# A tile arena moved by 56 columns, and another order of transposes and gate products at the end of an rwkv stage

## The reference

```
y = ((y - mean) * rsqrt(var + GN_EPS)).reshape(b, s, d) * ln_w + ln_b
bonus = sum(rh * kh * r_k, -1, keepdims=True) * vh
y = y + bonus.reshape(b, s, d)
return (y * g) @ w_o
```

## Time and profile before

| | |
|---|---|
| runs, median of three | 1237.35 us (1236.31 to 1237.88) |
| the profiled execution | 1236.65 us |
| its span | 1234.8 us |
| TensorE busy | 1221.0 us, 99% |
| VectorE, ScalarE, GpSimd busy | 538.0, 608.5, 776.7 us |
| instructions | 23237 |

### The profile page before, as it was taken

How to read it: one execution, slowest core, us unless ns; L and a number is a source line. 1 busy time by engine, 2 the same in 40 slices (tenths; PEclk the granted TensorE clock), 3 DMA queues, 4 the chain that set the end, 5 groups by cost and what they waited for, 6 DMA issues and landing times.

```text
span 1234.8 us, 23237 instructions
## 1 busy us (share of the span) xinstructions
PE 1221.0 (99%) x9698; PEld 1062.6 (86%) x9698; DVE 538.0 (44%) x819; ACT 608.5 (49%) x796; POOL 776.7 (63%) x200
## 2 busy tenths in 40 slices
PE   8999999999999999999999999999999999999998
PEld 7888887788988888899898888888888998888887
DVE  4432234655333333343523333348986573332233
ACT  7454443545554444585565445464422444554442
POOL 3988880153288888767369888843016525888884
PEclk9999999999999999999999999999999999999999
DMA  8655554253255555554235555542341133555551
GB/s 301 212 186 199 178 201 148 89 184 140 103 174 201 202 175 200 193 184 160 103 137 202 176 201 179 195 170 103 136 163 44 38 117 122 184 195 197 180 201 68
DMA packets 31020, 202.01 MB, mean 164 GB/s; under 512 B 3424, under 2 KB 5344, under 8 KB 7392
## 3 DMA queue, kind: packets, MB, share of 16 engines
q1 hardware_dynamic: 28064, 196.63, 45.2%
q10 hardware_dynamic: 2880, 4.26, 1.0%
HBM read 198.79 MB, written 2.10 MB: 163 GB/s over the span
## 4 chain that ended last, share of the span: by engine, by line
PE 95%; ACT 1%; POOL 1%; issue 1%; DVE 1%; DMA 1%; SPq 0%; POOLq 0%; DVEq 0%; ACTq 0%
PE psum L353 25%; PE psum L355 13%; PE psum L344 10%; PE psum L346 10%; PE psum L345 10%; PE psum L986 6%; PE psum L999 3%; PE psum L2992 2%; PE psum L3008 1%; POOL wlo L3371 1%; PE psum L2847 1%; PE psum L341 1%; PE psum L343 1%; PE psum L342 1%; PE psum L2962 1%
## 5 line engine op out<-in xcount | busy, mean ns | idle before, releaser
L3371 POOL TENSOR_TENSOR wlo<-raw,whi 128x2048 fp32r<-128x2048 f32 x160 | 734.3, 4595 | 289.7 <-ACT whi L314 244.3
L353 PE MATMUL psum<-f_both,whi 128*128 128x512 f32 x1408 | 497.3, 394 | 1.0 <-DVE wlo L699 1.0
L314 ACT ACTIVATE whi<-raw 128x2048 fp32r<-128x2048 f32 x160 | 306.3, 1915 | 223.1 <-PE psum L355 173.9
L355 PE MATMUL psum<-f_both,wlo 128*128 128x256 f32 x1408 | 397.4, 282 | 0.0
L353 PEld LDWEIGHTS psum<-f_both,whi 128*128 128x128 f32 x1408 | 264.4, 188 | 62.0 <-DVE wlo L699 1.6
L355 PEld LDWEIGHTS psum<-f_both,wlo 128*128 128x128 f32 x1408 | 264.7, 188 | 1.5
L344 PE MATMUL psum<-whi,ahi 128*128 128x512 f32 x352 | 137.2, 390 | 0.2 <-POOL wlo L3371 0.2
L346 PE MATMUL psum<-whi,alo 128*128 128x512 f32 x352 | 137.0, 389 | 0.0
L345 PE MATMUL psum<-wlo,ahi 128*128 128x512 f32 x352 | 137.0, 389 | 0.0
L909 DVE TENSOR_TENSOR psum<-psum,arena 128x512 f32<-128x512 f32 x43 | 30.1, 700 | 239.7 <-ACT arena L625 239.6
L925 DVE TENSOR_TENSOR alo<-arena,ahi 128x512 fp32r<-128x512 f32 x44 | 98.7, 2244 | 31.7 <-ACT ahi L858 31.7
(11 more groups left out here) (425 smaller groups left out, 1474.1 us busy)
## 6 DMA issues: line engine op xcount, KB each, us to landing
raw<-stream SPq DMA_DIRECT2D x182, 1024.0 KB, 4.8
con<-consts SPq DMA_DIRECT2D x1, 1376.0 KB, 14.2
x<-x_in SPq DMA_DIRECT2D x1, 1024.0 KB, 4.9
raw<-stream SPq DMA_DIRECT2D x2, 512.0 KB, 6.9
kept_x<-x ACTq DMA_DIRECT2D x1, 1024.0 KB, 3.9
x<-kept_x ACTq DMA_DIRECT2D x2, 512.0 KB, 4.7
out<-x SPq DMA_DIRECT2D x4, 256.0 KB, 2.0
arena<-gm_w_s ACTq DMA_DIRECT2D x1, 512.0 KB
```

Of the source, the lines that this page charges most:

```text
L314: nc.scalar.activation(whi[:, slot, :], raw[:, c % RAW, :], ACT.Copy).then_inc(high_made, 1)
L353: nc.tensor.matmul(psum[:, bank, :].rearrange("p (a n) -> p a n", a=2), whi[w], f_both[:, :, k, :], start=k == 0, stop=False, skip_group_c ...
L355: return nc.tensor.matmul(psum[:, bank, 0:TOK], wlo[w], f_hi[:, k, :], start=False, stop=k == KT - 1, skip_group_check=True)
L3371: nc.gpsimd.tensor_tensor(part(wlo[:, slot, :]), part(raw[:, c % RAW, :]), part(whi[:, slot, :]).bitcast(F32), ALU.subtract)\
```

## The change

Three edits. The unused columns ahead of the arena are 16 in place of 72, which puts it at byte 103968 of each partition. On VectorE `gated(3)` stands ahead of `y_low(2)`. On TensorE `turned(2)` stands amid the tiles of `out_tiles(1)`, which takes a list of tiles for this; each of the two calls waits for the same value of `rw_ylo`.

```diff
-        sb("up_to_line", [P, 72])
+        sb("up_to_line", [P, 16])
...
             whole(3)
+            gated(3)
             y_low(2)
-            gated(3)
             y_low(3)
...
-            def out_tiles(w):
+            def out_tiles(w, tiles=range(4)):
 
                 m, q = PASSES[w]
                 eng.wait_ge(s("rw_ylo"), w + 1)
-                return pair_tiles("rw_o", range(4 * q, 4 * q + 4), 0, m, last=KT - 1)
+                return pair_tiles("rw_o", [4 * q + k for k in tiles], 0, m, last=KT - 1)
...
             out_tiles(0)
-            out_tiles(1)
+            out_tiles(1, (0, 1))
             turned(2)
+            out_tiles(1, (2, 3))
             turned(3)
             out_tiles(2)
             out_tiles(3).then_inc(chunk_used, 2)
```

## The result

The changed kernel takes 1229.01 us (median of 6 runs, 1228.64 to 1231.48), the kernel before 1236.76 (6 runs): a ratio of 0.9941, interval [0.9928, 0.9954]. A second series gave 1230.23 against 1236.59, 0.9947 [0.9934, 0.9961]. The profiled execution took 1229.58 us, with a span of 1227.8.

A forecast was written before the change was run, and what follows sets the result against it. TensorE, busy 99% of the span, was taken as the bound. 2.17 + 1.54 - 0.70 + 0.35 = 3.36 us gained, the arena zero; from a median of 1237.35 to 1234.0 us, range 1231.0 to 1237.0.

The forecast's parts named there:

- Parts 1 and 2: End of rwkv: gated(3) ahead of y_low(2) on VectorE, turned(2) amid TensorE's second products; together 3.36 us earlier.
- last product: End of rwkv on TensorE: the stage's last product starts at 37.68 in place of 41.04.
- second products: End of rwkv: TensorE reaches these at 24.73 in place of 26.90, 2.17 us gained, and ends them at 30.41.
- first low part's product: First last_out product that waits for GpSimd's low part: that part is ready at 31.11, TensorE comes at 30.41.
- The new wait: TensorE, ahead of the first last_out product: 0.70 us of waiting for GpSimd's low part, which had cover before.
- the 1.54 us of the lower clock: Second products at the end of rwkv: 1.54 us read as the lower clock's price, gained once the idle time goes.
- Rival A: End of rwkv: TensorE's clock still falls, the 1.54 us come back, 2.2 gained in all, 1235.2 us; chance 0.10.
- Part 3: Arena 56 columns lower, at byte 103968, 32 past a multiple of 256: effect on reads taken as zero.
- rival C: FFN matmuls reading f_both: the arena move ends reads slowed by their place beside the weights; 1 ns gives 2.8 us; chance 0.09.
- The bound of 11.3 us: Limit on the arena's effect, either way: 4 ns on each of 2816 matmuls that read f_both; given little weight.
- the second objection: Caveat on the rows used for the arena's zero: their matmuls are not of the fp32r kind that f_both is.
- Both rows give no loss: Reason for little weight on the arena's bound: sums and lw, 32 bytes past a multiple of 256, read no slower.

The follow-up runs named there:

- e1: The kernel before with only the arena moved (16 unused columns in place of 72), orders unchanged: 1232.17 us, beside 1236.49 for the kernel before.
- e2: The changed kernel with 72 unused columns again, so only the new order of gated(3) and turned(2): 1233.74 us, 0.9975 of the kernel before.
- e7: The changed kernel with 56 unused columns added ahead of raw, weights 224 bytes up, arena back at byte 104192: 1229.97 us.
- e9: The changed kernel with 8 unused columns ahead of raw (weights 32 bytes up) and 8 ahead of the arena, which stays at byte 103968: 1234.86 us.
- e14: The changed kernel with 32 unused columns ahead of the arena in place of 16, distance of f_both to the weights +96 mod 256: 1230.3 us.
- e15: The changed kernel with 40 unused columns ahead of the arena in place of 16, distance of f_both to the weights +128 mod 256: 1238.5 us.
- e5: The changed kernel, arena still at byte 103968, but f_both alone 32 bytes below it at 103936: 1235.66 us.

## Why the prediction was wrong

- **Parts 1 and 2, the order: right for the profiled execution.** 3.36 were forecast up to the last product; the profile has 3.38. On the scale of the kernel before (add 2.46 to the times after): turned(2) 22.42 (forecast 22.41), turned(3) 24.26 (24.31), second products 24.61 (24.73), first low part's product 31.02 (31.11), last product 37.66 (37.68). The new wait is 0.56 by its row and 0.7 by the starts (forecast 0.70). Each single edit was forecast to end 0.9 later than both, and they gave 0.81 and 0.91. But the base of the forecast was luck in part: the 1.54 us of the lower clock were read from one execution, and e1, with the old orders and the same pause, ran without the fall. Then the order is worth 2.3 (21.82 against 19.52). The runs of e2 gained 2.75, between the two.
- **Rival A, the clock: not seen.** It stays at 1.00 there in the changed kernel; between the two profiled executions the 1.54 are all in the gain. Whether transposes count for the clock is not told by this: no pause was left in which it could have mattered.
- **Part 3, "I take zero": this step failed.** The term measured 4.3 us in e1: 4.8 gained in the FFN stages, 0.5 lost in the attention mixer. It is rival C, by the mechanism named there (a read that depends on its place beside the weights), at 1.8 ns per matmul and not 1, and I gave it 0.09.
- **Why it failed.** The earlier trace rows compare tiles 32 bytes past a line with tiles on one. That tests the place of an operand by itself, and e7 and e9 show that this is not the variable. The two groups differ in shape too (64 rows against 128), so that their 376 and 379 ns don't compare like with like. And they are plain float32 matmuls: L2847's start every 216 ns for 256 columns where the fp32r ones start every 118, so they may have room to hide what those can't; no run tested that. I wrote down the second objection and let the first pass. The bound of 11.3 us was wide enough; the range of 1231.0 to 1237.0 did not use it. "Both rows give no loss" bounds a loss in what they test, and says nothing of a gain.
- **What stays open.** Why the rate depends on the distance. In the kernel before the starts go 224, 234, 233 ns for L353 in a cycle of three pairs, in the changed one 228, 230 in a cycle of two, the same for all tiles. That, the two rates at one distance in e14 and e15, and the slow start of the down products behind the pairs, which read nothing of the arena, speak for the weight loads and the moving operand's reads getting in each other's way in a fixed beat rather than for single slow reads, but this is only argued. e7 and e9 moved not only the weights but all tensors ahead of the arena (raw, ahi, alo, x and the constants); the matmuls in question read whi and wlo alone of these, but ScalarE, GpSimd and the DMAs write whi, wlo and raw meanwhile, and no run tells these apart. What chooses between the two rates, and which reads slow the attention mixer down by 0.5 us, is open too.

## What to carry to other kernels

Where a kernel is bound by dense fp32r matmuls, the places of the two operands relative to each other are a parameter of their own: count the start-to-start time of matmuls in a steady stretch, try the eight offsets of 32 bytes within 256, look at each stretch and not only at the mean, and expect nothing from alignment, since here the aligned place took 3.7 ns a pair more than the best. A term whose nearest rows test another variable should keep its bound in the range, on both sides. For orders between engines, walking the chain with durations from one trace gave the result of another to 0.1 us; but a fall of the clock in that trace has to be seen in a second execution before its price is put into the gain (here 1.08 of 3.4 us hung on it). Two edits against one pause are worth less than their sum (2.3 against 1.5 and 1.4).

## What the hardware showed that was not expected

The mean rate of fp32r matmuls with a moving operand of 512 and 256 columns varied between 347.0 and 353.1 ns per pair with nothing changed but 32-byte steps in the distance of the operands; 768 columns at 2.4 GHz are 320 ns, so the excess over that goes from 27 to 33 ns. In the products of the first mixer and the attention stage that have `hhi` or `hlo` as the moving operand (L341 to L343), the start-to-start time of 256 columns went from 118.5 to 117.2 ns; e5, where `hhi` moved and `f_both` did not, has 117.5. A pause of 2.08 us of TensorE was followed by the lower clock in the profile before (0.62 in 1026.5 to 1031) and not in e1 (1.00 in 1025 to 1031), with the same instructions around it. The Trainium skill (TensorE: Matmul & The Clock Gate, Part 2: What happens when you issue a matmul) gives the moving operand and the weight loads a read port of SBUF each and says that loading the next weights takes nothing from the running matmul. By that rule one would not expect the distance between the two to matter; the 347.0 and 350.6 ns of e7 and e9, where only the distance tells, differ from that, and the measurement decides.
